# Decoder trunk in split float32: a ring of five weight units with the low parts written over the raw ones, x transposed in halves at stage boundaries, and another opening

## The chip, the core and the metric

The kernel runs on one core of a Trainium2 chip. The metric is the device time of one launch in microseconds (us), lower is better. PE is the matrix engine, ACT the scalar engine, DVE the vector engine, POOL the general one and SP the one that issues most transfers. Each engine works through its own instruction list in order and waits on semaphores. The matrix engine's clock has two levels, 2.4 GHz (shown as 1.0) and 1.2 GHz (0.5).

## The reference, cut to what matters

```python
for layer i in (0, 1):                       # 256 tokens x 1024, float32
    h += 0.5 * post_norm(SwiGLU_1(pre_norm(h)))      # 1024 -> 2 x 2816 -> 1024
    h += post_norm(mixer_i(pre_norm(h)))             # i = 0: gMLP + SSD ("hyb"); i = 1: latent attention ("mla")
    h += 0.5 * post_norm(SwiGLU_2(pre_norm(h)))
    h += post_norm(sigmoid(pre_norm(h) @ W_g) * (p[i] @ W_p))          # "ple"
def rmsnorm(x, g): return x * rsqrt(mean(x * x) + 1e-6) * g
```

Every norm is an RMS norm over the 1024 channels with its own weight; all weights are float32.

## The kernel before

Eight stages follow each other: ffn 0, hyb, ffn 1, ple, ffn 2, mla, ffn 3, ple. Their weights, 183 of them, come as one stream of **units** of 128 x 2048 numbers (1 MB). A unit is loaded by SP into `raw`, ACT writes its high part `WH` (a copy rounded to float32r, `split_hi`, L172), DVE the low part `WL` (raw minus high, `split_lo`, L178), and PE makes three products for each tile of it: high x high, low x high, high x low (`product`, L202 to L204). `raw`, `WH` and `WL` have three slots each (`RING`). A load of unit n waits until unit n-3 has been split; the split of unit n into `WH` waits until PE has used unit n-3 (`w_used`). Where the splits stand in ACT's and DVE's lists is written out by hand: `split_to(n)` splits all units up to n that haven't been split yet. In the text, u or m is the first unit of a stage.

The 256 tokens are two halves, t = 0 and t = 1. A unit is used for t = 0, then for t = 1; `w_used` counts the second. At a stage's start the order is staggered by `lagged`: (unit 0, t 0), (1, 0), (0, 1), (2, 0), (1, 1) ...

**A boundary** between stages, for each half t: ACT squares the stage's output (L271), DVE multiplies it by the post-norm weight (`gained`, L303), POOL adds up the mean (L308) and takes the power -1/2 (L311), DVE updates h (L317) and multiplies it by the next pre-norm weight (`normed`, L341) in two halves of the columns; PE transposes these (`transpose_x`, L354), ACT and DVE split them into `XH` and `XL` (L376, L381). For t = 0 both column halves are transposed in the middle of the stage's last unit (`next_x`, hook `middle` of `wide`), so that six products stand between them and the next stage. For t = 1 they stand in the second unit's and before the third group of products. After ple, whose results all come late, t = 0 is transposed after the last product. In ple, ACT loads the sigmoid table (`ple_act`) after its splits, and then takes t = 0's sigmoid (L762); PE's order there is both projections of p, then gates (0,0), (0,1), (1,0), (2,0), (3,0), (1,1), (2,1), (3,1), written (unit, t).

At the start of mla, `latents(t)` on DVE (L1785) follows squares on ACT and three small operations on POOL (L1890 to L1896); PE transposes the result (L1514).

**The opening**: POOL loads the first pre-norm weight as a broadcast to 128 rows (`QG`, 512 KB), SP x's first half, units 0 and 1, x's second half. PE runs 16 products on zeros, transposes x's first half once DVE has multiplied it by `QG`, and runs four more. Between blocks of an ffn stage PE, ACT and DVE run hardware loops of three rounds (`Fori`), and SP one over nearly the whole stream.

## Time and profile before

| | us |
|---|---|
| median of 3 runs | 1170.84 (1170.7 to 1171.07) |
| the profiled execution, its own time | 1170.79 |
| its span, first to last instruction | 1169.0 |
| PE busy | 1123.9 (96%) |
| DVE busy | 819.4 (70%) |
| ACT busy | 566.4 (48%) |
| POOL busy | 114.3 (10%) |
| read from HBM | 204.29 MB, 176 GB/s over the span |

The busy share of PE is nearly full, so that what an edit can win lies in PE's idle stretches; the rows below show those, and what ended each.

### The profile page before, as it was taken

What the parts mean: (1) busy time and instruction counts of PE and PEld (TensorE: products, weight loads), DVE (VectorE), ACT (ScalarE), POOL (GpSimd) and SP (SyncE); (2) the same over time, 40 slices, a digit from 0 to 9 for tenths busy, and PEclk for the clock granted to TensorE, in tenths of its full rate; (3) what the DMA queues carried; (4) which work ended last, traced back from release to release, by engine and by line L of the source; (5) the groups of instructions that cost most, each with busy time, mean ns of one, the idle gap of its engine ahead of it and who ended that gap; (6) DMA issues with size and microseconds to landing.
All of it is one profiled execution on the core that took longest, in us unless ns stands there. A gap on an engine that the chain in (4) does not pass through costs nothing.

```text
span 1169.0 us, 15408 instructions
## 1 busy us (share of the span) xinstructions
PE 1123.9 (96%) x5780; PEld 945.5 (81%) x5780; DVE 819.4 (70%) x1027; ACT 566.4 (48%) x671; POOL 114.3 (10%) x139
## 2 busy tenths in 40 slices
PE   7999999999899999999998999999989999999997
PEld 4888887788787788888777888887878878888875
DVE  5767777677786677677765777768865576776775
ACT  5444445567433644444555444445554554444453
POOL 4000000201600300000123000003100030000012
PEclk9999999999999999999999999999999999999999
DMA  7654554744342564645455655553622356555441
GB/s 269 239 216 173 186 183 146 283 163 158 112 163 108 186 219 180 213 172 190 154 195 197 216 176 183 184 212 108 216 108 73 109 188 216 178 182 205 166 169 54
DMA packets 30546, 206.05 MB, mean 176 GB/s; under 512 B 3504, under 2 KB 3536, under 8 KB 7072
## 3 DMA queue, kind: packets, MB, share of 16 engines
q1 hardware_dynamic: 27216, 194.00, 46.3%
q0 software_dynamic: 3280, 11.35, 3.0%
q8 instruction: 35, 0.57, 0.2%
q14 instruction: 15, 0.12, 0.0%
HBM read 204.29 MB, written 1.05 MB: 176 GB/s over the span
## 4 chain that ended last, share of the span: by engine, by line
PE 83%; DVE 9%; POOL 2%; ACT 2%; issue 1%; DMA 1%; DVEq 0%; POOLq 0%; ACTq 0%
PE PS L505 23%; PE PS L202 15%; PE PS L203 14%; PE PS L204 14%; PE PS L508 12%; DVE WL L178 4%; DVE hn L341 1%; DVE h L317 1%; DVE X L381 1%; DMA QG<-pre_g 1%; PE PS L354 1%; PE PS L1606 1%; PE PS L1607 1%; ACT junk L271 1%; ACT WH L172 0%
## 5 line engine op out<-in xcount | busy, mean ns | idle before, releaser
L178 DVE TENSOR_TENSOR WL<-raw,WH 128x2048 fp32r<-128x2048 f32 x182 | 418.1, 2299 | 147.2 <-ACT WH L172 147.1
L172 ACT ACTIVATE WH<-raw 128x2048 fp32r<-128x2048 f32 x183 | 349.0, 1908 | 133.5 <-PE PS L204 127.6
L505 PE MATMUL PS<-X,WH 128*128 128x512 f32 x1152 | 288.4, 392 | 0.0
L505 PEld LDWEIGHTS PS<-X,WH 128*128 128x128 f32 x1152 | 209.1, 189 | 39.0 <-DVE actb L619 0.2
L508 PEld LDWEIGHTS PS<-X,WL 128*128 128x128 f32 x1152 | 157.2, 190 | 11.2
L508 PE MATMUL PS<-X,WL 128*128 128x256 f32 x1152 | 160.6, 282 | 0.0
L202 PE MATMUL PS<-WH,X 128*128 128x512 f32 (+1 forms) x352 | 140.6, 400 | 9.1 <-DVE X L381 6.6
L204 PE MATMUL PS<-WL,X 128*128 128x512 f32 (+1 forms) x352 | 137.2, 390 | 0.0
L203 PE MATMUL PS<-WH,X 128*128 128x512 f32 (+1 forms) x352 | 137.1, 389 | 0.0
L202 PE MATMUL PS<-WH,BH 128*128 128x512 f32 x288 | 113.4, 394 | 0.0
L203 PE MATMUL PS<-WH,BL 128*128 128x512 f32 x288 | 112.5, 391 | 0.0
L204 PE MATMUL PS<-WL,BH 128*128 128x512 f32 x288 | 112.2, 389 | 0.0
L612 ACT ACTIVATE sgb<-sgb 128x256 f32<-128x256 f32 x72 | 30.1, 419 | 139.5 <-DVE sgb L608 139.5
L623 ACT ACTIVATE BH<-actb 128x256 fp32r<-128x256 f32 x72 | 30.0, 417 | 135.3 <-DVE actb L619 135.3
L308 POOL TENSOR_SCALAR stat<-stat 128x1 f32<-128x1 f32 x16 | 7.5, 466 | 859.6 <-ACT junk L271 859.6
L202 PEld LDWEIGHTS PS<-WH,X 128*128 128x128 f32 x352 | 66.4, 189 | 28.3 <-DVE WL L178 9.9
L204 PEld LDWEIGHTS PS<-WL,X 128*128 128x128 f32 x352 | 66.2, 188 | 13.8
L203 PEld LDWEIGHTS PS<-WH,X 128*128 128x128 f32 x352 | 66.4, 189 | 12.1
L599 DVE TENSOR_REDUCE gsum<-PS 128x256 f32<-128x512 f32 x72 | 49.5, 688 | 25.1 <-PE PS L508 25.1
L204 PEld LDWEIGHTS PS<-WL,BH 128*128 128x128 f32 x288 | 54.1, 188 | 11.6
L202 PEld LDWEIGHTS PS<-WH,BH 128*128 128x128 f32 x288 | 54.2, 188 | 11.4 <-DVE BL L627 1.2
L203 PEld LDWEIGHTS PS<-WH,BL 128*128 128x128 f32 x288 | 54.2, 188 | 9.8
(265 smaller groups left out, 1365.8 us busy)
## 6 DMA issues: line engine op xcount, KB each, us to landing
raw<-stream SPq DMA_DIRECT2D x183, 1024.0 KB, 4.8
QG<-pre_g POOLq DMA_DIRECT2D x8, 512.0 KB, 8.0
PG<-post_g POOLq DMA_DIRECT2D x8, 512.0 KB, 6.8
h<-x SPq DMA_DIRECT2D x2, 512.0 KB, 7.6
out<-h SPq DMA_DIRECT2D x4, 256.0 KB, 2.0
wsT<-gm_w POOLq DMA_DIRECT2D x1, 512.0 KB, 10.5
gm_g<-gm_g POOLq DMA_DIRECT2D x1, 512.0 KB, 11.0
gm_b<-gm_b POOLq DMA_DIRECT2D x1, 512.0 KB, 13.9
```

The costliest lines, as they stand in the source:

```text
L172: act.activation(WH[:, n % RING, :], raw[:, n % RING, :], ACT.Copy).then_inc(sem("w_hi"), 1)
L178: dve.tensor_tensor(WL[:, n % RING, :], raw[:, n % RING, :], WH[:, n % RING, :], ALU.subtract).then_inc(sem("w_lo"), 1)
L202: pe.matmul(out_ap, xh, wh, start=start, stop=False)
L203: pe.matmul(out_ap, xl, wh, start=False, stop=False)
L204: return pe.matmul(out_ap, xh, wl, start=False, stop=stop)
L271: act.activation(junk[:, t, half(b)], src, ACT.Square, scale=1.0 / 32 / post_factor(s), accum_out=col(s, t, POST_SQ + b)).then_inc(sem("po ...
L317: dve.scalar_tensor_tensor(h[:, t, half(b)], hn[:, t, half(b)], col(s, t, POST_RS), h[:, t, half(b)], ALU.mult, ALU.add).then_inc(sem("h_n ...
L505: pe.matmul(PS[:, bank, :], wh[:, kt, cols], X[:, kt, :, :].rearrange("p a n -> p (a n)"), start=kt == 0, stop=False)
L508: ins = pe.matmul(PS[:, bank, 0:SEQ], wl[:, kt, cols], XH[:, kt, :], start=False, stop=kt == KT - 1)
L599: return dve.tensor_reduce(dst, PS[:, bank, :].rearrange("p (a n) -> p n a", a=2), mybir.AxisListType.X, ALU.add)
L612: act.activation(sgb[:, v % 2, :], sgb[:, v % 2, :], ACT.Silu).then_inc(sem("b_silu"), 1)
L623: act.activation(BH[:, v % SLOTS, :], actb[:, v % 2, :], ACT.Copy).then_inc(sem("b_hi"), 1)
```

## The change

It does five things.

- **Ring.** Five slots instead of three; `WL` lies on the same addresses as `raw`, and DVE writes the low part over the raw one. A load of unit n now waits until PE has used unit n-5; the splits wait for the load alone. To make room `junk` is halved and `cmask` and `zeros` are moved, with waits that keep their users apart. The hardware loops are written out.
- **Boundaries.** The two transposes of t = 0 stand each before one pair of k-tiles of the last unit's second half. The stagger has a lead of two units: (0,0), (1,0), (2,0), (0,1), (3,0), (1,1), (2,1), (3,1), and t = 1 is transposed within (2,0). Units m and m+1 are split before the boundary's work on t = 0, m+2 before that on t = 1. The mean goes from POOL to DVE, behind `gained` (`post_mean`), and POOL keeps the power.
- **ple.** PE's order becomes projection t 0, gate (0,0), projection t 1 with the transposes of x in it, gates (1,0), (2,0), (3,0), (0,1), (1,1), (2,1), (3,1). ACT splits two units more ahead of its table load.
- **mla.** DVE's half splits of unit 2 (the other half was POOL's) become a whole split on DVE ahead of `latents(0)`; two splits stand ahead of `latents(1)`.
- **Opening.** x is transposed as it is loaded. The norm weight comes as a column per k-tile (`qg_cols`, 4 KB), and ACT and DVE apply it while they split (four instructions for each half of the columns instead of one). Units 0 and 1 are loaded and split in halves. Seven products on zeros, and later eight.

```diff
-RING = 3
+RING = 5
...
         raw = place("raw", [P, RING, UNIT])
+        WL = place("WL", [P, RING, UNIT], f32r, offset=base)
         WH = place("WH", [P, RING, UNIT], f32r)
-        WL = place("WL", [P, RING, UNIT], f32r)
...
-        junk = place("junk", [P, 2, D])
+        junk = place("junk", [P, D])
...
-        def load_unit(sp, n, k=None, step=0):
+        def load_unit(sp, n):
             if n >= RING:
-                sp.wait_ge(sem("w_hi"), unit_at(n - RING + 1, k, step))
-                sp.wait_ge(sem("w_lo"), unit_at(n - RING + 1, k, step))
+                sp.wait_ge(sem("w_used"), n - RING + 1)
...
+            sp.dma_start(raw[:, n % RING, :], a["stream"][n, :, :]).then_inc(sem(f"raw{n % RING}"), 16)
...
-            if n >= RING:
-                act.wait_ge(sem("w_used"), unit_at(n - RING + 1, k, step))
-            act.activation(WH[:, n % RING, :], raw[:, n % RING, :], ACT.Copy).then_inc(sem("w_hi"), 1)
+            act.wait_ge(sem(f"raw{n % RING}"), 16 * (n // RING + (1 if n % RING > 1 else 0)))
+            act.activation(WH[:, n % RING, :], raw[:, n % RING, :], ACT.Copy).then_inc(sem("w_hi"), 1)
...
+        def lagged(units, lead=1):
...
+            for j in range(len(units) + lead):
+                if j < len(units):
+                    order.append((units[j], 0))
+                if j >= lead:
+                    order.append((units[j - lead], 1))
...
             for c in range(2):
-                if c and middle is not None:
-                    middle()
                 for q in range(2):
+                    if c and middle is not None:
+                        middle(q)
...
-            dve.wait_ge(sem("post_sq"), 4 * s + 2 * t + b + 1)
+            if stages[s][0] != "ple":
+                dve.wait_ge(sem("post_sq"), 4 * s + 2 * t + b + 1)
...
+        def post_mean(dve, s, t):
...
+            dve.tensor_scalar(col(s, t, POST_RS), col(s, t, POST_SQ), col(s, t, POST_SQ + 1),
+                              col(s, t, POST_EPS) if stages[s][0] == "ffn" else EPS, ALU.add, ALU.add)\
+               .then_inc(sem("post_ms"), 1)
...
         def post_inverse_rms(pool, s, t):
-            pool.wait_ge(sem("post_sq"), 4 * s + 2 * t + 2)
-            link(pool, "pool_chain", pool.tensor_scalar(col(s, t, POST_RS), col(s, t, POST_SQ), col(s, t, POST_SQ + 1),
...
+            pool.wait_ge(sem("post_ms"), 2 * s + t + 1)
...
+            for b in range(2):
+                gained(dve, s, t, b)
+            post_mean(dve, s, t)
+            dve.wait_ge(sem("post_rs"), 2 * s + t + 1)
...
-                return lambda: transpose_x(pe, s + 1, 0)
+                return lambda half: transpose_x(pe, s + 1, 0, (half,))
...
+        def first_x_high(act, t, a_):
+            if (t, a_) == (0, 0):
+                act.wait_ge(sem("qg_cols"), 16)
+            act.wait_ge(sem("x_tr"), 2 * t + a_ + 1)
+            for q in range(4):
+                kt = 4 * a_ + q
+                ins = act.activation(XH[:, kt, tok(t)], PS[:, x_bank(0, t, a_), q * P:(q + 1) * P], ACT.Copy,
+                                     scale=qg_cols[:, kt:kt + 1])
...
+        def opening_act(act, done):
+            act.wait_ge(sem("consts"), 1)
+            first_x_high(act, 0, 0)
+            first_part_hi(act, 0, 0)
+            first_x_high(act, 0, 1)
+            first_part_hi(act, 0, 1)
+            pre_square(act, 0, 0)
+            first_part_hi(act, 1, 0)
+            first_x_high(act, 1, 0)
+            first_x_high(act, 1, 1)
+            first_part_hi(act, 1, 1)
...
         def boundary_dve(dve, s, done, split_to):
             m = first[s] if s < NS else n_units
+            split_to(m + 1)
             behind(dve, s - 1, 0)
...
-            split_to(m)
             x_low(dve, s, 0)
-            split_to(m + 1)
+            if stages[s][0] != "mla":
+                split_to(m + 2)
             behind(dve, s - 1, 1)
             x_low(dve, s, 1)
             if stages[s][0] != "mla":
-                split_to(m + 2)
+                split_to(m + 3)
...
+        def opening_dve(dve, done):
+            first_x_low(dve, 0, 0)
+            first_part_lo(dve, 0, 0).then_inc(sem("w_lo_half"), 1)
+            first_x_low(dve, 0, 1)
+            first_part_lo(dve, 0, 1).then_inc(sem("w_lo"), 1)
+            first_x_low(dve, 1, 0)
...
+            order = lagged(range(4), 2) if s else [(j, t) for j in range(4) for t in range(2)]
...
-                    if (j, t, q) == (1, 0, 3):
-                        transpose_x(pe, s, 1, (0,))
+                    if s and (j, t) == (2, 0) and q % 2 == 0:
+                        transpose_x(pe, s, 1, (q // 2,))
...
+                    if s == 0 and (j, t, q) == (0, 0, 2):
+                        transpose_x(pe, 0, 1)
...
-            with pe.Fori(0, 3) as k:
...
+            for p in range(7):
+                n = u + 8 + 3 * p
+                ffn_block_pe(pe, f, 2 + 2 * p, n)
+                ffn_block_pe(pe, f, 3 + 2 * p, n + 1)
...
-            for j, t in [(0, 0), (0, 1), (1, 0), (2, 0), (3, 0), (1, 1), (2, 1), (3, 1)]:
...
+            projected(0)
+            gate(0, 0)
+            projected(1, lambda half: transpose_x(pe, s, 1, (half,)))
+            for t in range(2):
+                for j in range(1 - t, 4):
+                    gate(j, t)
...
         def ple_act(act, s, done, split_to):
-            split_to(first[s] + 4)
+            split_to(first[s] + 6)
             load_table(act, ACT.Sigmoid)
 
         def ple_dve(dve, s, done, split_to):
-            split_to(first[s] + 4)
+            split_to(first[s] + 5)
...
+            split_to(u + 2)
             dve.wait_ge(sem("ml_cg"), 32)
             latents(0)
-            dve.wait_ge(sem("ml_half"), 1)
-            split_lo_half(dve, u + 2, 1).then_inc(sem("w_lo"), 1)
-            done[0] = u + 3
             latents_low(0)
-            split_to(u + 3)
+            split_to(u + 4)
             latents(1)
-            split_to(u + 4)
+            split_to(u + 5)
             latents_low(1)
...
+            sp.dma_start(qg_cols[:, :], a["pre_g0"]).then_inc(sem("qg_cols"), 16)
+            load_part(0, 0)
+            load_part(0, 1)
             sp.dma_start(h[:, 1, :], a["x"][tok(1), :]).then_inc(sem("x_loaded1"), 16)
+            load_part(1, 0)
+            load_part(1, 1)
+            for n in range(2, n_units):
                 load_unit(sp, n)
...
-            pool.dma_start(QG[:, :], a["pre_g"][0, :].partition_broadcast(P)).then_inc(sem("qg"), 16)
+            pool.memset(zeros[:, :], 0.0).then_inc(sem("zeros"), 1)
...
+            pe.wait_ge(sem("zeros"), 1)
+            idle_products(pe, 7)
             pe.wait_ge(sem("consts"), 1)
-            idle_products(pe, 16)
...
                 if s == 0:
-                    idle_products(pe, 4)
+                    idle_products(pe, 8)
```

On ACT, in the program's opening (X is the split x, WH the high weights, junk takes squares). Before:

```order
L172 ACT_TABLE_LOAD
L172 ACTIVATE WH<-raw 128x2048 [waits raw0]
L376 ACTIVATE X<-PS 128x4x128 [waits x_tr] x2
L172 ACTIVATE WH<-raw 128x2048 [waits raw1]
L283 ACTIVATE junk,stat<-h 128x1024 [waits x_loaded0]
```

Of the change:

```order
L404 ACT_TABLE_LOAD [waits x_tr,qg_cols]
L404 ACTIVATE X<-PS,qg_cols 128x128 [waits consts]
L404 ACTIVATE X<-PS,qg_cols 128x128 x3
L443 ACTIVATE WH<-raw 128x1024 [waits w_part0]
L404 ACTIVATE X<-PS,qg_cols 128x128 [waits x_tr]
L404 ACTIVATE X<-PS,qg_cols 128x128 x3
L443 ACTIVATE WH<-raw 128x1024 [waits w_part1]
L287 ACTIVATE junk,stat<-h 128x1024 [waits x_loaded0]
```

The table load, which waited for nothing, now stands behind the waits for the first transpose and for the weight's columns.

On ACT, through the ple stage (p_hi and x done; gsb holds the sigmoid, ple_gate is a gate's product). Before:

```order
L376 ACTIVATE X<-PS 128x4x128 [waits x_tr] x2
L283 ACTIVATE junk,stat<-h 128x1024 [waits h_new]
L172 ACTIVATE WH<-raw 128x2048 [waits w_used,raw0]
L386 ACT_TABLE_LOAD
L386 ACTIVATE mark<-nhalf 128x1
L762 ACTIVATE gsb<-PS,stat 128x512 [waits pre_rs,ple_gate] x2
```

Of the change:

```order
L389 ACTIVATE X<-PS 128x4x128 [waits x_tr] x2
L287 ACTIVATE junk,stat<-h 128x1024 [waits pre_sq,h_new]
L164 ACTIVATE WH<-raw 128x2048 [waits raw1]
L164 ACTIVATE WH<-raw 128x2048 [waits raw2]
L164 ACTIVATE WH<-raw 128x2048 [waits raw3]
L419 ACT_TABLE_LOAD
L419 ACTIVATE mark<-nhalf 128x1
L817 ACTIVATE gsb<-PS,stat 128x512 [waits pre_rs,ple_gate] x2
```

Ahead of the table load and the sigmoid stand three splits, of units u+4, u+5 and u+6, where one stood.

On DVE, at the start of mla (cn are the normalised latents, krT the rotary keys). Before:

```order
L1803 COPY krT<-PS 64x128
L178 TENSOR_TENSOR WL<-raw,WH 128x2048 [waits w_hi]
L1785 SCALAR_TENSOR_TENSOR cn<-PS,msm,cg 128x256 [waits ml_rs]
L1786 SCALAR_TENSOR_TENSOR cn<-PS,msm,cg 128x128
L1773 TENSOR_TENSOR ra<-PS,cosT 128x32
```

Of the change:

```order
L1870 COPY krT<-PS 64x128
L171 TENSOR_TENSOR WL<-raw,WH 128x2048 [waits w_hi] x2
L1852 SCALAR_TENSOR_TENSOR cn<-PS,msm,cg 128x256 [waits ml_rs]
L1853 SCALAR_TENSOR_TENSOR cn<-PS,msm,cg 128x128
L1840 TENSOR_TENSOR ra<-PS,cosT 128x32
```

Two splits stand between the first half's keys and the second half's latents, where one stood.

## Rows read from the trace of the kernel before

**Rows 1.** Page, part 4: the chain that ended last, shares by engine.

```profile
PE 83%; DVE 9%; POOL 2%; ACT 2%; issue 1%; DMA 1%; DVEq 0%; POOLq 0%; ACTq 0%
```

**Rows 2.** Waits of PE: for whom; us in total, times, longest us.

```profile
PE PS L354 <- DVE hn L341: 6.9, 12, 2.7
...
PE PS L202 <- DVE X L381: 6.6, 9, 1.4
...
PE PS L202 <- issue: 3.8, 3, 1.6
```

**Rows 3.** Windows: span, busy of PE, PEld, DVE, ACT, POOL; PEclk; DMA share, GB/s.

```profile
40.00:199.00 159.00, 159.00 (x837) 136.64 (x836) 115.00 (x126) 69.38 (x70) 2.55 (x3) 1.00 0.51 187
...
322.10:325.40 3.30, 3.30 (x18) 3.30 (x17) 3.30 (x2) 0.00 (x0) 0.09 (x1) 0.50 0.45 164
```

**Rows 4.** Timeline of the opening: start us, us, engine, line, [idle before].

```profile
0.80 1.28 ACT L172 ACT_TABLE_LOAD   x1 [0.80 <-PEq L2146]
...
4.27 5.45 PE L2031 MATMUL PS<-zeros 128*128 128x512 bf16 x16 [4.27 <-POOL cmask L1999]
...
7.61 1.91 ACT L172 ACTIVATE WH<-raw 128x2048 fp32r<-128x2048 f32 x1 [5.53 <-DMA raw<-stream]
...
10.43 1.29 DVE L341 TENSOR_TENSOR hn<-h,QG 128x512 f32<-128x512 f32 x2 [10.43 <-DMA QG<-pre_g]
...
14.67 0.47 PE L202 MATMUL PS<-WH,X 128*128 128x512 f32 x1 [1.37 <-DVE X L381]
...
38.64 0.61 PE L480 MATMUL PS<-ident,stat 128*128 128x128 f32 x4
```

**Rows 5.** Lines by form: xcount | busy us, mean ns | idle before.

```profile
L178 DVE TENSOR_TENSOR WL<-raw,WH 128x2048 fp32r<-128x2048 f32 x182 | 418.1, 2299 | 147.2 <-ACT WH L172 147.1
...
L317 DVE SCALAR_TENSOR_TENSOR h<-hn,stat,h 128x512 f32<-128x512 f32 x32 | 23.7, 746 | 5.3 <-POOL stat L311 5.3
...
L1786 DVE SCALAR_TENSOR_TENSOR cn<-PS,msm,cg 128x128 f32<-128x128 f32 x2 | 0.7, 342 | 0.0
...
L1693 ACT ACTIVATE junk<-PS,stat 128x128 f32<-128x128 f32 x2 | 0.7, 358 | 0.0
```

**Rows 6.** Timeline, ffn 1 to ple to ffn 2: PE, ACT and POOL.

```profile
572.91 0.57 POOL L311 TENSOR_TENSOR stat<-stat,nhalf 128x1 f32<-128x1 f32 x1
...
575.53 0.60 PE L354 MATMUL PS<-ident,hn 128*128 128x128 f32 x4
...
583.27 0.47 PE L202 MATMUL PS<-WH,p_hi 128*128 128x512 f32 x1 [1.56 <-issue]
...
600.00 0.69 ACT L762 ACTIVATE gsb<-PS,stat 128x512 f32<-128x512 f32 x1 [3.31 <-PE PS L204]
...
609.33 1.04 PE L354 MATMUL PS<-ident,hn 128*128 128x128 f32 x8
...
611.43 0.47 PE L202 MATMUL PS<-WH,X 128*128 128x512 f32 x1 [1.07 <-DVE X L381]
...
619.17 1.12 PE L354 MATMUL PS<-ident,hn 128*128 128x128 f32 x4 [2.71 <-DVE hn L341]
...
639.78 0.60 PE L480 MATMUL PS<-ident,stat 128*128 128x128 f32 x4
```

**Rows 7.** Page, part 6: DMA issues, KB each, median us to landing.

```profile
raw<-stream SPq DMA_DIRECT2D x183, 1024.0 KB, 4.8
```

**Rows 8.** Timeline, start of mla: POOL and PE.

```profile
818.97 2.12 POOL L1891 TENSOR_SCALAR msm<-msm 128x1 f32<-128x1 f32 x1
...
824.29 0.65 PE L1514 MATMUL PS<-ident,cn 128*128 128x128 f32 x4 [1.15 <-DVE cn L1792]
```

**Rows 9.** Timeline, mla to ffn 3: PE.

```profile
938.41 0.60 PE L354 MATMUL PS<-ident,hn 128*128 128x128 f32 x4
...
966.79 0.61 PE L480 MATMUL PS<-ident,stat 128*128 128x128 f32 x4
```

More of the change, by code:

```diff
@@ L667, in ffn_act @@
-            block_high(act, f, 16)
-            split_to(u + 32)
-            block_silu(act, f, 17)
-            block_high(act, f, 17)
-            split_to(u + 33)
+            for p in range(8):
+                n, v = u + 8 + 3 * p, 2 + 2 * p
+                last = p == 7
+                split_to(n + 3)
+                block_silu(act, f, v)
+                split_to(n + 4)
+                block_high(act, f, v)
+                block_silu(act, f, v + 1)
+                if not last:
+                    split_to(n + 5)
+                block_high(act, f, v + 1)
+                if p == 6 and s + 1 < NS and stages[s + 1][0] == "ple":
+                    act.wait_ge(sem("p_loaded"), 16 * (stages[s + 1][1] + 1))
+                    act.activation(p_hi[:, :, :], p_raw[:, :, :], ACT.Copy).then_inc(sem("p_hi"), 1)
```

444 lines of the change are left out of this document (216 added, 228 removed).

## The prediction, made before the changed kernel had run

> **What bounds the kernel now.** I read the page first: PE is busy in 96% of the span, and the chain of waits runs over PE for 83% and over DVE for 9% [rows 1]. So PE sets the pace and only its idle stretches can be won. Next the table of waits shows who keeps PE idle: DVE's `hn` ahead of the transposes of x (6.9 us in 12 waits), DVE's low x ahead of products (6.6 in 9), and `issue` (3.8 in 3, the longest 1.6) [rows 2]. Then a window over the inside of an ffn stage: PE is busy 159.00 of 159.00 us at full clock [rows 3]. All that can move lies in the opening, at the stage boundaries and at the start of mla. Last I read the timelines of those places. The profiled execution took 1170.79 us by its own time, with a span of 1169.0; the median shown is 1170.84, so a sum made on the one holds for the other.
>
> **Ring and unrolled loops: 0.** DVE needs 2299 ns for each of 182 splits [rows 5], and a transfer takes 4.8 us to land [rows 7]; a window of an ffn stage has room for both, since PE never waited in it [rows 3]. Five slots hide what is hidden already. That the loads now wait for PE's use, and no longer for DVE's split, costs nothing while units come one after another in PE's order. The written-out loops bring more instructions to fetch, which nothing shows as a wait of PE in 40 to 199 us. By the Trainium skill, "Runtime: NRT & Kernel Launch", section "Instruction fetch mechanics", a taken branch breaks the sequential prefetch, so that writing loops out would gain something; the row, where PE crosses such branches with no idle time, gives 0, and the row decides.
>
> **Opening: -3.9.** Before, ACT's first split waits for its unit (7.61), DVE's `hn` waits for `QG` until 10.43, and the first real product starts at 14.67 [rows 4]. The change needs neither. PE's zeros shrink from sixteen in 5.45 us to seven, 7 x 0.34 = 2.4 us from about 2.5, and x is transposed straight from its load. Of its landing I have only the end of POOL's constants, 4.27, for which PE waited [rows 4]; with the zeros and four transposes behind it I take 5.7. ACT then pays its table load, 1.28 us [rows 4], which now stands behind the waits for x and the columns. It makes high x in four instructions of 128 columns; the nearest row, 358 ns, has an accumulator beside it [rows 5], I take 0.28: 1.1 us. A part of unit 0 is half of 1.91 [rows 4], 1.0. DVE's four are of the kind of 342 ns [rows 5], 0.3 each: 1.2, and its half split is half of 2299 ns, 1.2. From 5.7: 7.0, 8.1, then DVE's x at about 9.3 and its split at 10.5. First product about 10.5 against 14.67, which is 4.2 earlier; products then wait some 0.3 more for halves in small pieces (ACT's 1.1 and 1.0 for each part stand against 1.4 of products), so -3.9. I look for it in the rs transposes of ffn 0, at 38.64 before [rows 4], at 34.75 after. Bounds: +/-2.1 about it. If x lands as late as the weights' first unit does (7.61, [rows 4]), the gain is 1.8; if the table load slips in before x and the small instructions cost half, 6.
>
> **ffn to ple: -1.9, twice.** The first transpose of t = 0 starts at 575.53, PE waits 1.56 us at 583.27 ahead of p's second projection [rows 6], and has some 0.8 of short waits, a part of the sums in rows 2; the gates end at 609.33, 33.8 us after 575.53 [rows 6]. In the new order gate (0,0) stands there instead, and the transposes of t = 1 stand inside the second projection. I count all of 1.56 and 0.8, less 0.4 for a wait ahead of the new gate (0,0): 31.9 to the end of the gates. Bounds: 0 (the wait of 1.56 is for something that the order leaves as it was) and -2.4.
>
> **ple to ffn 2: +6.2.** This is the term that speaks against the change. Before the sigmoid's table load ACT now splits units u+4, u+5 and u+6 where one split stood. Unit u+6 lies in the slot of u+1, and its load waits until PE has used u+1, the first gate unit, for both halves: the end of gate (0,1), the seventh piece in PE's new order. All times now from the stage's first transpose, which is 575.53 before [rows 6]: about 3.3 until p's first projection, seven pieces of twelve products in the 2.73 us that twelve take there, and four pairs of transposes, make 23.6. With 4.8 to land [rows 7] that is 28.4. Behind it stand, all on the way to t = 0's new h: the split on ACT 1.9 (to 30.3), the table load and its first use 1.3 and 0.2 (31.8), half of the sigmoid 0.7 (32.5), DVE's products and `gained` 1.3 each (35.1), mean 0.3, power 0.6 (36.0, [rows 6]), update and norm of a half, 2 x 0.75 (746 ns, [rows 5]). So the first `hn` comes at 37.6, and PE has ended the gates at 31.9: 5.7 us idle. First product at 39.8, against 35.9 before (611.43 less 575.53, [rows 6]). Before, the wait there was 1.07 [rows 6], because t = 0's sigmoid ran at 600.00, when the gates had still 9 us to go. The second half's chain starts behind the first's on DVE, which leaves a second wait, of about 3.2 ahead of (2,0) in the next stage, where 2.71 stood [rows 6]. After an idle time of this size the clock is granted at 0.5 for 3.3 us [rows 3], a loss of 1.65; behind the first wait the second one takes it up, and behind the second it was there before too. So 3.9 + 0.5 - 0.1 = 4.3 from first transpose to rs transposes, 64.25 before (639.78 less 575.53, [rows 6]) and 68.55 after; -1.9 of it is the item above, so the stall alone is +6.2. Bounds: if the split of u+6 doesn't stand in the way, 0; if the load takes twice the median to land, +11.0.
>
> **Other boundaries: -1.4.** Six products stood between t = 0's transposes and the next stage; now one half's transposes come earlier and the other's later, and two units of t = 0 come first. DVE has more room for t = 1 but takes over the mean, 0.5 to 0.9 us on the chain, because POOL did it beside `gained`. I work out hyb's next stage by the same sums: +0.1 at ffn to hyb, where about 1.3 us of waiting moves to (2,0); -0.4 at hyb to ffn 1, where only short waits go; -1.1 at mla to ffn 3 (28.38, from 938.41 to 966.79 [rows 9], becomes 27.3, since both of its waits go). Bounds: each wait left in place 0, or each mean paid in full, 3 x 0.9 = +2.7.
>
> **mla's start: +1.2.** Two DVE splits stand back to back ahead of `latents(1)`. Before, one POOL operation there of 128x1 took 2.12 us under a DVE split, and PE waited 1.15 us at 824.29 [rows 8]. With two splits all three POOL operations of t = 1 fall under one: latents come 1.7 later, and PE's wait is about 2.85; some of it comes back since DVE's half split of unit 2 no longer waits for POOL's half. Bounds: 0 (POOL gets in between the splits) to +2.3 (a whole split). By the Trainium skill, "SBUF — State Buffer", section "Who interferes with whom", a DVE instruction with two SBUF inputs and a GpSimd one that reads SBUF exclude each other, and the second is blocked until the first has finished; this speaks against the change here, and the trace agrees: 2.12 us [rows 8]. Without that rule the three POOL operations would take at most three times the 0.57 of a power [rows 6] beside the splits and the term would be 0.
>
> **Sum.** -3.9 - 3.8 + 6.2 - 1.4 + 1.2 = -1.7, from 1170.8: **1169.1 us**, taken as 1169.0. The unknown sizes of the opening (2.1), the ple stall (about 2) and the others (about 1) leave its own range at 1166.5 to 1171.7. A measurement of this kernel tells 0.2%, 2.3 us, from no change: faster is below 1168.5, slower above 1173.2.
>
> **Rivals.**
> - *The ple stall does not happen* (0.22). The load of u+6 is issued in time, or t = 0's chain had enough cover: the six us stay won, about 1163. For it: t = 0's sigmoid at 600.00 left 9 us of cover. Against it: ACT is in order, and the split stands ahead of the table load in its list.
> - *The load of u+6 lands late* (0.10), the case that ends on the other side. The broadcasts of the norm weights are under way there, and the four slots ahead of it refill from the same queue. At twice the median, 9.6 us, every part of the stall is 4.8 later: 1173.8. It is slower by over 0.2% from a landing of 8.9 us on. Against: the median is 4.8 [rows 7].
> - *Short waits at boundaries halve the clock* (0.06). Five new waits of 1.1 to 1.4 us at (2,0), each followed by a stretch like that of rows 3, five times 1.65 = +8.3: 1177. Against: the wait of 1.56 at 583.27 [rows 6] is of that length.
> - *Instructions arrive late after writing the loops out* (0.05): one wait for `issue` like the longest, 1.6 [rows 2], in each of the four written-out ffn stages, +6.4: 1175.4. Against: PE idle time of 0 in rows 3.
> - *The opening gains little* (0.07): x or the columns land late, -1.5 in place of -3.9: 1171.5.
>
> The forecast's own case has 0.50: faster 0.20, same 0.28, slower 0.02. With the first rival all on the side of faster, the second to fourth mostly slower, the last one same: **faster 0.42, same 0.35, slower 0.23**. Range 1163.5 to 1173.5: it takes in nearly all of the first rival's case and the near end of the late load, and leaves out the far ones.
>
> **What would show it.** Opening: first real product at 10 to 11, rs transposes of ffn 0 near 34.8; if the table load stands after the transpose, that step is right. ple: ACT idle ahead of the split of u+6 and waiting for the load, then PE idle for 5 to 6 us ahead of t = 0's transposes with the clock at 0.5 behind it. If ACT's third split there starts without a wait on the DMA, the largest term is wrong and the time is near 1163. Boundaries: waits of 1.1 to 1.4 at (2,0) and none at the first product. mla: about 2.9 us ahead of the second half's latents, with POOL's small operations lengthened. Ring: no idle time of PE between 40 and 199. Everything falls if PE's busy sum itself moves, since only idle time is counted here.

## The result, and the profile after

| | us |
|---|---|
| changed kernel, median of 4 runs | 1163.64 (1163.13 to 1165.92) |
| kernel before, beside it on the same chip, 4 runs | 1170.95 (1170.7 to 1171.5) |
| ratio, 95% interval | 0.9941 (0.9923 to 0.9958) |
| profiled execution, span | 1161.7 (before 1169.0) |

The kernel is 7 us faster, 0.6%, clear of the 0.2% that a measurement tells from no change. The time lies at the low end of the range, by the first rival's number of 1163, but that rival's mechanism did not happen: the stall behind ple is there, as large as forecast. Other terms were wrong, in both directions. PE's waits in the changed kernel, as in [rows 2] (for whom; us in total, times, longest):

```profile
PE PS L367 <- DVE hn L351: 10.2, 7, 5.8
PE PS L1580 <- DVE cn L1859: 4.2, 2, 3.1
...
PE PS L189 <- DVE WL L479: 2.8, 1, 2.8
```

The waits for low x ahead of products, 6.6 us in 9 [rows 2], have gone. Those for `hn` have become fewer and longer, and the new longest is 5.8.

I cut both spans at the same transposes, and took the differences. "M" is the first transpose of a stage's x. "H" is the first transpose of an ffn stage's inner activations (`act_h`); in both kernels it starts 6.04 us behind the stage's rs transposes, at which the prediction made its sums, so the differences compare.

| from, to | before | after | difference | forecast |
|---|---|---|---|---|
| start, H of ffn 0 | 44.68 | 41.14 | -3.5 | -3.9 |
| H to M, inside the four ffn stages | 618.5 | 617.4 | -1.05 | 0 |
| M hyb, M ffn 1 | 187.0 | 189.1 | +2.1 | +0.1 |
| M ffn 1, H ffn 1 | 34.5 | 32.6 | -1.9 | -0.4 |
| M ple, H ffn 2 | 70.3 | 71.5 | +1.2 | +4.3 |
| M mla, M ffn 3 | 138.0 | 138.8 | +0.7 | +1.2 |
| M ffn 3, H ffn 3 | 34.4 | 32.5 | -2.0 | -1.1 |
| M of the last ple, end | 41.6 | 38.8 | -2.8 | -1.9 |
| sum | | | -7.3 | -1.7 |

Not all of the 7.3 is idle time. PE's busy sum, which the prediction took as fixed, fell from 1123.9 to 1120.8 though only five of its 5780 instructions, products on zeros, have gone. In ffn 1 between M and H it went from 32.53 to 31.50, the idle time from 1.96 to 1.07. By windows (span, busy of PE, PEld, DVE, ACT, POOL; PEclk; DMA share, GB/s), before, then after:

```profile
386.51:421.00 34.49, 32.53 (x156) 25.83 (x155) 24.45 (x23) 19.23 (x24) 8.51 (x11) 1.00 0.59 206
```

```profile
384.62:417.19 32.57, 31.50 (x154) 26.03 (x155) 21.04 (x22) 17.62 (x23) 6.74 (x10) 1.00 0.59 229
```

**Opening.** Start, us, engine, line, [idle before]; before in [rows 4]:

```profile
4.63 1.08 PE L367 MATMUL PS<-ident,h 128*128 128x128 f32 x8
5.38 1.28 ACT L404 ACT_TABLE_LOAD   x1 [5.38 <-PE PS L367]
...
6.68 1.14 ACT L404 ACTIVATE X<-PS,qg_cols 128x128 fp32r<-128x128 f32 x4
...
10.26 0.47 PE L189 MATMUL PS<-WH,X 128*128 128x512 f32 x1 [2.82 <-DVE WL L479]
...
35.10 0.61 PE L557 MATMUL PS<-ident,stat 128*128 128x128 f32 x4
```

The table load stands behind x's first transpose, and the first product comes at 10.26, where the chain of six pieces gave 10.5. The rs transposes stand at 35.10 against the 34.75 forecast.

**Behind ple.** ACT first, then PE; before in [rows 6]:

```profile
599.82 1.92 ACT L164 ACTIVATE WH<-raw 128x2048 fp32r<-128x2048 f32 x1 [9.47 <-DMA raw<-stream]
601.76 1.28 ACT L419 ACT_TABLE_LOAD   x1
...
603.16 1.25 ACT L817 ACTIVATE gsb<-PS,stat 128x512 f32<-128x512 f32 x2
```

```profile
608.80 1.11 PE L367 MATMUL PS<-ident,hn 128*128 128x128 f32 x4 [5.81 <-DVE hn L351]
...
619.68 0.63 PE L367 MATMUL PS<-ident,hn 128*128 128x128 f32 x4 [0.57 <-DVE hn L351]
```

ACT waits 9.47 us for u+6's load, and the sigmoid waits behind it. It lands at 599.8, 28.3 us after M (571.54; forecast 28.4); `hn` releases PE 37.3 us after M (37.6), after 5.81 us of idle time (5.7). The second wait is 0.57, not 3.2. Between the two the clock is at its lower level (0.51) for 7.0 us, where 3.3 were forecast, by the same kind of window:

```profile
608.80:615.80 7.00, 6.61 (x19) 4.94 (x20) 5.82 (x7) 2.65 (x5) 0.00 (x0) 0.51 0.00 0
```

**mla's start**, DVE, POOL and PE; before in [rows 8]:

```profile
808.02 2.16 POOL L1965 TENSOR_SCALAR msm<-msm,stat 128x2 f32<-128x2 f32 x1
...
812.25 0.66 PE L1580 MATMUL PS<-ident,cn 128*128 128x128 f32 x4 [1.13 <-DVE cn L1859]
...
814.55 4.52 DVE L171 TENSOR_TENSOR WL<-raw,WH 128x2048 fp32r<-128x2048 f32 x2
814.80 2.12 POOL L1960 TENSOR_SCALAR msm<-msm 128x1 f32<-128x1 f32 x1
817.01 2.63 POOL L1963 TENSOR_TENSOR msm<-msm,nhalf 128x2 f32<-128x2 f32 x1
...
822.04 0.66 PE L1580 MATMUL PS<-ident,cn 128*128 128x128 f32 x4 [3.08 <-DVE cn L1859]
```

In the second half two of POOL's four small operations are held under the two splits, each until its split has ended, and PE's wait is 3.08 (forecast 2.85). In the first half the whole split that now stands ahead of `latents(0)` holds another one (2.16 us), and that wait has grown from 0.31 to 1.13. The prediction had no term for it.

**hyb's end**, DVE and PE. This is no term of the prediction:

```profile
360.98 6.69 DVE L171 TENSOR_TENSOR WL<-raw,WH 128x2048 fp32r<-128x2048 f32 x3
367.58 1.22 DVE L1336 TENSOR_TENSOR CL<-PS,CH 128x1024 fp32r<-128x1024 f32 x1
...
368.86 0.50 PE L189 MATMUL PS<-WH,CH 128*128 128x512 f32 x1 [1.19 <-DVE CL L1336]
```

With five slots most of the hand-written `split_to` calls in hyb and mla were moved on by one unit, and here three splits stand ahead of `CL` where two stood.

### The profile page after: what moved, and what is told of

The parts are those of the page before. It is cut to its first block, busy times and chain, and to the rows that moved or that the text cites. A ratio compares the mean times of both kernels' runs of the same rounds, so it can differ in the third digit from the quotient of the medians.

```text
span 1161.7 us, 14173 instructions
## 1 busy us (share of the span) xinstructions
PE 1120.8 (96%) x5775; PEld 946.7 (81%) x5775; DVE 816.9 (70%) x1053; ACT 561.6 (48%) x685; POOL 99.8 (9%) x121
## 3 DMA queue, kind: packets, MB, share of 16 engines
HBM read 203.77 MB, written 1.05 MB: 176 GB/s over the span
## 4 chain that ended last, share of the span: by engine, by line
PE 60%; DVE 9%; ACT 3%; POOL 3%; issue 2%; DMA 0%; DVEq 0%; POOLq 0%
PE PS L582 17%; PE PS L189 10%; PE PS L191 10%; PE PS L190 10%; PE PS L585 9%; DVE WL L171 3%; PE PS L367 1%; ACT WH L164 1%; DVE h L328 1%; DVE hn L351 1%; PE PS L1672 1%; PE PS L1673 1%; DVE hn L308 1%; POOL hn L1493 0%; DVE ca L1272 0%
## 5 line engine op out<-in xcount | busy, mean ns | idle before, releaser
L171 DVE TENSOR_TENSOR WL<-raw,WH 128x2048 fp32r<-128x2048 f32 x181 | 413.5, 2290 | 177.6 <-ACT WH L164 177.1
L164 ACT ACTIVATE WH<-raw 128x2048 fp32r<-128x2048 f32 x181 | 344.7, 1908 | 131.5 <-DMA raw<-stream 131.3
L582 PEld LDWEIGHTS PS<-X,WH 128*128 128x128 f32 x1152 | 209.1, 189 | 38.8
L322 POOL TENSOR_TENSOR stat<-stat,nhalf 128x1 f32<-128x1 f32 x16 | 8.9, 555 | 883.0 <-DVE stat L315 883.0
L671 DVE TENSOR_REDUCE usum<-PS 128x256 f32<-128x512 f32 x72 | 49.7, 691 | 41.5 <-PE PS L585 41.5
L189 PE MATMUL PS<-WH,CH 128*128 128x512 f32 x128 | 52.7, 412 | 4.8 <-DVE CL L1943 2.9
```

Source lines behind the costliest of these rows:

```text
L164: act.activation(WH[:, n % RING, :], raw[:, n % RING, :], ACT.Copy).then_inc(sem("w_hi"), 1)
L171: dve.tensor_tensor(WL[:, n % RING, :], raw[:, n % RING, :], WH[:, n % RING, :], ALU.subtract).then_inc(sem("w_lo"), 1)
L189: pe.matmul(out_ap, xh, wh, start=start, stop=False)
L582: pe.matmul(PS[:, bank, :], wh[:, kt, cols], X[:, kt, :, :].rearrange("p a n -> p (a n)"), start=kt == 0, stop=False)
L671: return dve.tensor_reduce(dst, PS[:, bank, :].rearrange("p (a n) -> p n a", a=2), mybir.AxisListType.X, ALU.add)
```

## The experiments

All start from the changed kernel unless said otherwise. Times are medians; since not all ran on the same chip, each comes with its ratio to the kernel before on its own chip, whose 95% interval is about 0.0015 to either side (changed kernel: 0.9941).

**Fewer splits ahead of the sigmoid (e1_ple).**

```diff
-            split_to(first[s] + 6)
+            split_to(first[s] + 5)
             load_table(act, ACT.Sigmoid)
...
+            after_ple = s < NS and stages[s - 1][0] == "ple"
-            split_to(m + 1)
+            split_to(m if after_ple else m + 1)
             behind(dve, s - 1, 0)
...
+            if after_ple:
+                split_to(m + 1)
             x_low(dve, s, 0)
```

> The changed kernel, but in ple ACT splits only two units ahead of the sigmoid's table load, and both engines split the next stage's second unit (u+6) behind the first half's boundary work instead of ahead of it. Theory (the in-order wait of ACT for u+6's load delays the sigmoid): the 5.8 us of PE idle time ahead of the first x transpose behind ple and the 2.8 us that the half clock cost behind it both go; the second half becomes the later one, with some 2.5 us of idle time in (2,0) and 1.7 us of clock: from the ple stage's first transpose to ffn 2's first h transpose 71.5 us in the changed kernel becomes about 66.5, total about 1158.7. Rival (the table load, or DVE's own work, is what is late): the idle time stays over 4 us and the total within 1 us of 1163.6. Rival (supply of units is short there): the wait moves to the low parts of u+6 or u+7 and the total falls by less than 2 us.

Measured 1156.97, ratio 0.9883. From ple's M to ffn 2's H it is 64.9 us (71.5 in the changed kernel). PE:

```profile
606.12 0.47 PE L189 MATMUL PS<-WH,X 128*128 128x512 f32 x1 [1.77 <-DVE X L394]
...
613.58 0.63 PE L367 MATMUL PS<-ident,hn 128*128 128x128 f32 x4 [1.74 <-DVE hn L351]
```

```profile
606.20:609.50 3.30, 3.30 (x15) 2.71 (x16) 3.30 (x4) 0.79 (x3) 0.00 (x0) 1.00 0.41 169
614.40:617.70 3.30, 3.30 (x18) 2.71 (x17) 2.12 (x4) 2.08 (x4) 0.12 (x1) 1.00 0.00 0
```

The cause holds: with the load out of the way of the sigmoid the 5.81 are gone. The stage gives 6.6 where 5.0 were expected, since behind the two waits of 1.77 and 1.74 the granted clock stays at 1.00.

**PE's old order in ple (e9_pleorder).**

```diff
-            def gate(j, t):
+            def gate(j, t, middle=None):
...
             projected(0)
-            gate(0, 0)
-            projected(1, lambda half: transpose_x(pe, s, 1, (half,)))
-            for t in range(2):
-                for j in range(1 - t, 4):
-                    gate(j, t)
+            projected(1)
+            gate(0, 0, lambda half: transpose_x(pe, s, 1, (half,)))
+            for j, t in [(0, 1), (1, 0), (2, 0), (3, 0), (1, 1), (2, 1), (3, 1)]:
+                gate(j, t)
```

> The changed kernel with PE's order of before in ple (both projections first, then gate (0,0) with the second half's transposes in it, then (0,1)). Theory (the stall behind ple comes from where gate (0,1) stands, since the load of u+6 waits for its end): (0,1) is then the fourth piece and not the seventh, the load is asked for 8 us earlier, and the 5.8 us of idle time and the 2.8 us of clock behind ple mostly go (3.5 of both may stay as the second half's wait); but the waits of before inside ple, 1.56 and 0.8, come back in both ple stages, +2.4 each. Total about 1163.6 - 5.3 + 4.8 = 1163. Rival (the order in ple costs nothing, the wait of 1.56 for issue was about something else): the last stage takes 38.8 us from its first transpose as in the changed kernel, and the total is about 1158. Rival (the table load or the splits before it are the cause, not the load): idle time behind ple stays near 5.8, total 1168.

Measured 1161.24, ratio 0.9919. PE:

```profile
578.71 0.47 PE L189 MATMUL PS<-WH,p_hi 128*128 128x512 f32 x1 [1.42 <-issue]
586.04 0.50 PE L189 MATMUL PS<-WH,X 128*128 128x512 f32 x1 [0.72 <-DVE X L394]
```

The ACT list is untouched, three splits ahead of the table load, and the stall is gone: it comes from where gate (0,1) stands. The old order's own waits are back (1.42 and 0.72), and the last stage, which has nothing behind it, takes 40.9 us against 38.8: the new order is worth 2.1 us there. From ple's M to ffn 2's H this kernel takes 67.0 us against 71.5. So if the new order wins the same 2.1 in the first ple stage too, it loses 6.6 behind it, as much as e1_ple won back.

**Four slots (e6_ring4).**

```diff
-RING = 5
+RING = 4
```

> The changed kernel with four slots instead of five. Theory (in ple the load of u+6 is asked for when PE has used the unit RING earlier, and the sigmoid stands behind it): that load is asked for one gate piece later, so the idle time behind ple grows from 5.81 to about 8.5 us, total +2.7, about 1166.4, and nothing changes inside the ffn stages. Rival (a deep ring is what carries the whole change): PE gets waits for low parts inside the ffn stages and the total is above 1170. Rival (the stall has another cause): idle time stays at 5.8.

Measured 1265.76, ratio 1.0814. My theory fell as a forecast of the time: it named one stall, and there are many. The wait behind ple is 8.43, close to its 8.5, but the total is that of the first rival, and there are waits inside the ffn stages (`BL`):

```profile
PE PS L367 <- DVE hn L351: 22.1, 7, 8.4
PE PS L189 <- DVE BL L699: 16.9, 4, 4.3
PE PS L189 <- DVE X L394: 12.7, 5, 4.1
```

PE's idle time accounts for some 69 of the 102 us. The other 33 are in its busy sum (1154.1 against 1120.8), at a mean granted clock of 0.964 against 0.991. The splits stand in ACT's and DVE's lists up to four units ahead of PE, and a slot is now free only when PE has used it. ACT's waits for loads of units, first in the changed kernel, then in this one:

```profile
ACT WH L164 <- DMA raw<-stream: 131.3, 47, 9.5
```

```profile
ACT WH L164 <- DMA raw<-stream: 302.5, 90, 14.5
```

I read it so: with four slots such a split waits for a load that can't be asked for yet, and what stands behind it in the list, `hn`, low x or `BL`, waits with it. That this is so at each of the places was not looked at. The changed kernel's lists need five slots; an ordering of the splits made for four was not tried.

**The mean on POOL (e5_mean).**

```diff
                 gained(dve, s, t, b)
-            post_mean(dve, s, t)
...
-            pool.wait_ge(sem("post_ms"), 2 * s + t + 1)
+            pool.wait_ge(sem("post_sq"), 4 * s + 2 * t + 2)
+            link(pool, "pool_chain", pool.tensor_scalar(col(s, t, POST_RS), col(s, t, POST_SQ), col(s, t, POST_SQ + 1),
+                                                        col(s, t, POST_EPS) if stages[s][0] == "ffn" else EPS,
+                                                        ALU.add, ALU.add))
```

> The changed kernel, but the mean of the post-norm is POOL's again (beside DVE's gained) and not DVE's behind gained. Theory (the mean on DVE stands on the chain of each half): each half's h comes about 0.4 us earlier, the waits of 1.03 ahead of (2,0) fall to 0.6, that of 0.47 behind hyb goes, total -1.5, about 1162.1. Rival (POOL's small operations are held up by DVE's work, which is why the mean is better on DVE): POOL's mean lengthens to 0.7 us or more under DVE's multiplications, the waits stay or grow, total 1163.6 to 1165.

Measured 1158.18, ratio 0.9900, which is 4.8 us less by ratio; the span of the profile is 5.8 us shorter. Boundary from ffn 0 to hyb, second half, first the changed kernel, then this one:

```profile
201.01 1.28 DVE L308 TENSOR_TENSOR hn<-PS,PG 128x512 f32<-128x512 f32 x2
202.21 0.27 DVE L315 TENSOR_SCALAR stat<-stat 128x1 f32<-128x1 f32 x1
202.55 0.55 POOL L322 TENSOR_TENSOR stat<-stat,nhalf 128x1 f32<-128x1 f32 x1 [8.63 <-DVE stat L315]
203.14 0.75 DVE L328 SCALAR_TENSOR_TENSOR h<-hn,stat,h 128x512 f32<-128x512 f32 x1 [0.66 <-POOL stat L322]
```

```profile
199.02 1.90 POOL L322 TENSOR_SCALAR stat<-stat 128x1 f32<-128x1 f32 x1 [5.68 <-ACT junk L269]
200.59 1.28 DVE L308 TENSOR_TENSOR hn<-PS,PG 128x512 f32<-128x512 f32 x2
...
201.78 0.74 DVE L331 SCALAR_TENSOR_TENSOR h<-hn,stat,h 128x512 f32<-128x512 f32 x1
```

Both sides of my expectation were half right. POOL's mean is held up, 1.90 us under a split, but it starts early enough: it ends at 200.9, while DVE is still at `gained`, and the power is ready when DVE is done. On DVE mean and power stand one after the other behind `gained`: from its end at 202.3 to the update at 203.14 pass 0.85 us, and h comes 1.36 later (1.24, counted from each kernel's own M of hyb). Where PE waited 1.03 to 1.06 ahead of the second half's transposes it waits 0.12 to 0.14 now, and the 0.47 at the first transposes behind hyb has gone.

**Old stagger in the ffn stages (e8_lead1).**

```diff
-            order = lagged(range(4), 2) if s else [(j, t) for j in range(4) for t in range(2)]
+            order = lagged(range(4), 1) if s else [(j, t) for j in range(4) for t in range(2)]
...
+                if s and (j, t) == (0, 1):
+                    transpose_x(pe, s, 1, (1,))
...
-                    if s and (j, t) == (2, 0) and q % 2 == 0:
-                        transpose_x(pe, s, 1, (q // 2,))
+                    if s and (j, t, q) == (1, 0, 3):
+                        transpose_x(pe, s, 1, (0,))
```

> The changed kernel with the ffn stages' stagger of before: a lead of one unit, and the second half transposed inside (1,0) and ahead of (0,1). Theory (the lead of two units is what the boundaries won): in the three ffn stages behind another stage the second half is wanted 0.7 us earlier and the waits there grow by 1 to 1.5 us each, total about 1167.5. Rival (the won time is from the earlier splits and the transposes of the first half one column half at a time): waits only shift, total within 1 us of 1163.6.

Measured 1167.39, ratio 0.9968, as expected. From M to H ffn 1 takes 33.7 us (32.6 in the changed kernel, 34.5 before) and ffn 3 33.7 (32.5; 34.4). The wait ahead of the transposes grows from 1.03 to:

```profile
394.39 0.66 PE L367 MATMUL PS<-ident,hn 128*128 128x128 f32 x4 [1.62 <-DVE hn L351]
```

So the lead of two units carries 1.2 of the 1.9 us that each of these boundaries won, of which 0.6 is this wait.

**mla's splits (e2_mla, e10_mla2).** First, one DVE split of the two goes behind the second half's latents:

```diff
-            split_to(u + 4)
+            split_to(u + 3)
             latents(1)
             split_to(u + 5)
             latents_low(1)
```

> The changed kernel, but one DVE split instead of two ahead of the second half's latents in mla; the other follows behind them. Theory (POOL's small operations are blocked while DVE splits, so each further split costs about one more blocked operation): PE's wait for the second half's latents falls from 3.08 to about 1.15 us, total -1.9, about 1161.7. Rival (the units are needed early, so that the split is missed later): the wait of 1.15 is back, but a wait for a low part of some 1.5 us appears within the next two units, total within 0.5 of 1163.6.

Measured 1165.4, ratio 0.9962, if anything slower. PE:

```profile
819.54 0.66 PE L1580 MATMUL PS<-ident,cn 128*128 128x128 f32 x4 [1.14 <-DVE cn L1859]
824.90 0.50 PE L189 MATMUL PS<-WH,cTH 128*128 128x512 f32 x1 [3.32 <-DVE krT L1870]
```

The first half of the theory holds in the profile, 3.08 becomes 1.14, and the next wait takes it: 1.12 becomes 3.32, because two splits now stand ahead of the keys. Neither theory had named that wait. By ratio the kernel is 2.4 us slower than the changed one; its profile is that of the fastest of six executions and does not show where. Then u+3, u+4 and u+5 one by one:

```diff
-            split_to(u + 4)
+            split_to(u + 3)
             latents(1)
-            split_to(u + 5)
+            split_to(u + 4)
             latents_low(1)
+            split_to(u + 5)
             turn(0)
```

> The changed kernel with one DVE split ahead of mla's second latents, one ahead of their low parts and one ahead of the rotary turns, where two, one and none stood. Theory (an extra split anywhere between the latents and the keys is paid in full): both the 3.08 ahead of the second latents and the 3.3 ahead of the second keys, which stood there when two splits had been put between, are now 1.1, total -1.9, about 1161.7. Rival (this stage is bound by the supply of units): a wait for a low part of 1 to 2 us comes within the next four units, total within 0.5 of 1163.6.

Measured 1162.6, ratio 0.9934. PE:

```profile
815.14 0.80 PE L189 MATMUL PS<-WH,cTH 128*128 128x512 f32 x1 [1.06 <-DVE krT L1870]
824.07 0.50 PE L189 MATMUL PS<-WH,cTH 128*128 128x512 f32 x1 [1.13 <-DVE krT L1870]
```

No wait for the second latents is left and that for the keys is 1.13. Of the 1.9 about 1.0 is seen: M of mla to M of ffn 3 takes 137.8 us against 138.8, because in this profile products from 815.1 to 818.3 run at half clock (the first of them takes 0.80 us, and 0.50 in the changed kernel), which they did not in the changed kernel's. That PE comes later for it also hides a part of the wait for the latents. The time alone doesn't separate this run from the changed kernel.

The other runs show how far a single wait can be trusted here. e1_ple and e4_open have the changed kernel's mla, word for word, and their wait for the second latents is 1.53 and 1.56 us, that of e5_mean and e9_pleorder 3.33. In e4_open:

```profile
812.93 0.79 PE L189 MATMUL PS<-WH,cTH 128*128 128x512 f32 x1 [1.07 <-DVE krT L1871]
820.38 0.66 PE L1581 MATMUL PS<-ident,cn 128*128 128x128 f32 x4 [1.56 <-DVE cn L1860]
```

The transposes stand 24.67 us behind M in e4_open, e1_ple and the changed kernel alike. The latents come when DVE and POOL have done them; PE, at half clock before them, only waits less.

**hyb's end (e3_hyb).**

```diff
             split_to(u + 24)
-            split_to(u + 25)
             out_low(1, 8, "hy_yhi", "hy_ylo")
```

> The changed kernel, but at hyb's end DVE makes two splits instead of three ahead of the last low part of y (CL); the third follows behind it. Theory (the hand-written place of the splits, moved on by one unit with the longer ring, costs PE the wait of 1.19 us for CL): that wait goes, total about 1162.4. Rival (DVE's list is just as full behind it): the split then stands ahead of the boundary's work and the first transposes behind hyb wait 1 us or more longer than the 0.47 they do, total within 0.3 of 1163.6.

Measured 1162.67, ratio 0.9931. The wait of 1.19 is gone, and the 0.47 behind it has stayed (0.45), so the rival fell in its place. In time it is within the intervals. Its profile takes 1.2 us longer from M of hyb to the transposes at 321.46 (320.29 in the changed kernel), with half clock over 317 to 324 where that one had it over 318.5 to 322.5, and this hides the gain.

**Early table load (e4_open).**

```diff
             act.wait_ge(sem("consts"), 1)
+            load_table(act, ACT.Copy)
             first_x_high(act, 0, 0)
```

> The changed kernel, but ACT loads its table with a dummy copy as soon as the constants are there, ahead of the wait for x's first transpose. Theory (the table load stands on the opening's chain): the first product starts about 1.2 us earlier, at 9.0 instead of 10.26, and as x's second half lands at 10.2 about 0.7 of it is left at ffn 0's first h transpose (40.4 instead of 41.1), total about 1162.9. Rival (the halves of units 0 and 1 and x's second half set the pace by their landing): first product earlier, but the h transpose within 0.2 of 41.1 and the total unchanged.

Measured 1162.65, ratio 0.9934. PE's first product is at 9.24; then:

```profile
11.36 1.09 PE L367 MATMUL PS<-ident,h 128*128 128x128 f32 x8 [0.49 <-DVE WL L480]
...
14.99 0.47 PE L189 MATMUL PS<-WH,X 128*128 128x512 f32 x1 [1.15 <-DVE X L413]
```

ffn 0's H stands at 40.18 here, 41.14 in the changed kernel, and 41.20 and 40.74 in the two combined kernels below, where ACT waits 1.29 and 1.07 us for the load of a half unit. So the theory holds where the halves land in time. The eight other experiments that keep the changed opening have their H at 40.9 to 41.9, so it is worth 0 to 1 us, and the time alone doesn't show it.

**The old kernel with its loops written out (e7_unroll).** `with pe.Fori(0, 3) as k` becomes `for k in range(3)`, on ACT, DVE and SP too.

> The kernel before, with its hardware loops written out on PE, ACT, DVE and SP, and nothing else changed. In the two traces an ffn stage's inside takes 154.55 us before (from its first h transpose to the next stage's first x transpose, in three of four stages, 154.83 in the first) and 154.35 after. Theory (the loops' branches cost PE that 0.2 per stage): 154.35 here too, total 1170.0. Rival (it is the ring or the order of the splits): 154.55 and 1170.8. Rival (more instructions to fetch cost something): above 154.6.

Measured 1170.82, ratio 1.0003 (0.9994 to 1.0013). From H to M ffn 1, 2 and 3 take 154.5 us as before. Writing the loops out does nothing; the 0.2 us per stage of the changed kernel belongs to something else (ring or order of splits), which stays open.

**All of it (b2, then b1).** b2 has the mean on POOL, two splits at hyb's end, e10's mla, the early table load, and in ple one split less ahead of the table load with ffn 2's first transposes inside the last gate. b1 is the same but for ple, which is that of e1_ple. The main line that b2 alone has:

```diff
-                    gate(j, t)
+                    gate(j, t, next_x(pe, s) if (j, t) == (3, 1) else None)
```

> All in one: the mean on POOL, two splits at hyb's end, mla as in the run before this one, the early table load in the opening, and in ple one split less ahead of the table load with the next stage's first transposes inside the last gate, u+6 and u+7 split behind the first half's boundary work. If the gains add (5.5 for the mean, 6.7 for ple, 1.0 each for hyb and the opening, 1.9 for mla, some 0.8 for the transposes inside the gate): about 1147 to 1148. Rival (the waits behind ple and in mla take up part of what comes earlier, as they are set by chains that start at a fixed work of DVE): about 1151.

> The kernel of the run before (all five edits), but with ple's end as in the first experiment: the next stage's first transposes stand behind the last gate again, and u+6 is split ahead of the low part of x. Theory (one wait of 3.98 us behind ple costs more than two of 1.8, as the clock falls behind it): from ple's first transpose to ffn 2's first h transpose 64.9 us, as in the first experiment, in place of 67.97, with waits of about 1.8 and 1.7 and the granted clock at 1.0 behind both; total 3 us less than 1152.2, about 1149. Rival (the half clock of that run behind the wait was chance, and the stage costs what its chain costs): within 1 us of 1152.2.

b2: 1152.21 (1149.68 to 1153.47), ratio 0.9839 (0.9825 to 0.9852). b1: 1150.0 (1148.26 to 1150.79), ratio 0.9821 (0.9808 to 0.9834). The wait behind ple, b2, then b1, with windows behind it:

```profile
609.97 1.09 PE L369 MATMUL PS<-ident,hn 128*128 128x128 f32 x4 [3.98 <-DVE hn L353]
```

```profile
610.00:616.00 6.00, 6.00 (x19) 4.99 (x20) 2.73 (x5) 2.20 (x5) 0.91 (x1) 0.52 0.00 0
```

```profile
601.24 0.47 PE L189 MATMUL PS<-WH,X 128*128 128x512 f32 x1 [1.88 <-DVE X L396]
608.76 0.63 PE L369 MATMUL PS<-ident,hn 128*128 128x128 f32 x4 [1.81 <-DVE hn L353]
```

```profile
609.50:612.80 3.30, 3.30 (x18) 2.73 (x17) 2.12 (x4) 2.07 (x4) 0.20 (x1) 1.00 0.00 0
```

From M of ple to H of ffn 2 b2 takes 67.97 us and b1 64.66. The second half's `hn` comes 41.9 and 41.3 us after M, nearly the same; it is DVE's list that sets it. Transposing earlier only turned two waits of 1.8 into one of 3.98, and behind that the clock stands at 0.52 for 6 us. The 3.3 us are those of one pair of profiles. In time the two intervals overlap, and b2's profile is that of its slowest execution: two of its five took 1149.7 us, as little as b1's. So the rival of b1's expectation, that this half clock was chance, is not ruled out.

b2 is slower than both sides of its expectation, b1 within 1 us of its theory. b1 is 1.8% faster than the kernel before and 1.2% faster than the changed one. The single gains (4.8 and 6.8 us by ratio for mean and ple, about 1 each for the three others) sum to about 14, and 0.9941 less 0.9821 is 14 us. They add as far as the intervals tell; each of the three small ones is within its own interval of nothing.

## Why the prediction was right, and where not

It said "faster" as the likeliest sign and 1169.0 in a range of 1163.5 to 1173.5. The sign was right, and 1163.64 is just inside the range, but the forecast's own case (1166.5 to 1171.7) does not hold it. By its steps:

- **Opening, -3.9: right.** -3.5, with the first product, the table load's place and the chain of small instructions as worked out.
- **ple to ffn 2, +6.2, and its cause: right.** Landing, sigmoid and first `hn` came within 0.4 us, e1_ple and e9_pleorder show the cause, and undoing it gives 6.6.
- **The second wait behind it, 3.2, and the clock: wrong**, and 3.1 us of the miss. The prediction's own numbers put the second `hn` some 50 us after M (39.8, two units of 2.73, 1.65 lost to the clock, 3.2 of wait). It came after 48.1. Behind the first wait the clock was low for 7.0 us of work and not 3.3, so that PE lost 3.4 there and came to the second `hn` with only 0.57 left to wait. With that there is no second fall of the clock.
- **Order in ple, -1.9 twice: right mechanism.** e9_pleorder gives 2.1.
- **Other boundaries, -1.4: the step that failed most.** ffn 1 won 1.9 and ffn 3 2.0 where I had 0.4 and 1.1, and ffn 0 to hyb some 1.1 where I had +0.1. I moved the wait for low x (0.75 to 0.85, a part of the 6.6 in [rows 2]) on to (2,0). It was gone: by then the second half needed only 1.0, and that was mostly the mean's. e8_lead1 shows 1.2 of each as the lead's. The prediction also counted idle time alone and said that all falls if PE's busy sum moves. It did: in ffn 1 idle time gives only 0.9 of the 1.9, the other 1.0 is PE's busy time as the profile counts it, and over the span 3.1, of which 1.05 inside the four ffn stages. Why PE takes less busy time for the same products stays open.
- **The mean on DVE, "0.5 to 0.9 us on the chain": mis-sized.** It is about 1.2 us in the half shown, and 4.8 us of the time by ratio in the whole kernel. I compared the operation's length with POOL's. What counts is where it starts: POOL's runs beside DVE's split, ahead of `gained`.
- **mla's start, +1.2: right place and cause**, 2.85 forecast and 3.08 measured for the wait. The trace agrees with the rule that the prediction cites from the Trainium skill, "SBUF — State Buffer", section "Who interferes with whom": two POOL operations took 2.12 and 2.63 us under the splits. They were two of four, not "all three". The first half's wait grew by 0.8 as well, and the boundary ahead gained 2.0; for neither was there a term, and together they left +0.7 in sum.
- **hyb, 0: wrong, +3.2 behind its boundary.** I took the ring as costless and read the moved `split_to` calls at the places that the change's description names, not in hyb. Three splits ahead of `CL` cost PE the 1.19 (e3_hyb). The 0.47 at the boundary stayed there with the split moved and went with the mean (e5_mean). At 266.3 and 284.7 PE paused for 0.3 and 0.6 us more than between other products, the second with a wait of 0.45 for a low part; no experiment touched these, and the remaining 0.7 is not placed.
- **Ring and loops, 0: right for the loops** (e7_unroll) and inside the ffn stages, where PE still has no idle time. For the ring as a whole the reason was wrong: the prediction let the new wait, for PE's use, cost nothing and took the depth as no matter. With four slots the same lists cost 102 us (e6_ring4), and the `split_to` calls moved for five cost hyb its term.

The errors partly cancelled: the boundaries with the one ahead of mla (5.6), the second wait (3.1), the ffn stages' insides (1.05) and the last ple (0.9) gave about 11 us more than forecast, hyb, mla's waits and the opening took 5 back. That the sum landed in the range is luck of signs.

## What to carry to other kernels

Where splits, table loads and activations stand in one in-order list, read for each early load what frees its slot, and put nothing urgent behind it. Where a list's calls are shifted by one unit, count at every place how many now stand in a row. A small operation belongs on the engine that can start it early, even if it runs slower there. Whether an idle stretch cut in two is cheaper than one is not settled by these runs: it was so in two profiles, and the clock also fell behind short waits elsewhere.

## What the runs showed that I had not expected

- Behind ple the granted clock stayed at 1.00 behind waits of 1.7 to 1.9 us (e1_ple, b1), and fell to 0.51 and 0.52 for 6 to 7 us behind 5.81 and 3.98. It is not the length alone: in mla it fell to 0.50 for 3.2 us behind waits of 1.21 and 1.06 within 2.4 us (e10_mla2), and did not behind 1.13 and 1.07 at the same place in the changed kernel.
- The same places do not always lose the same: behind the waits of 3.5 us in hyb and 2.7 in ffn 2 the old kernel's profile lost 1.7 us each to the half clock, that with the loops written out nothing (span 1166.0 and mean clock 0.999, against 1169.0 and 0.995), while their medians agree. A single profile of this kernel is good to some 3 us in its span, and a wait behind a stretch of half clock can be 1.5 us shorter with the chain unchanged. The time from one transpose to another tells more than a wait.
- POOL's mean took 1.90 us under a DVE split and was still the better choice.
